# The turning quarter's forms in a Winograd MLP: two loads of 1 MB per form in place of four of 512 KB

## What is computed

```python
    h = rmsnorm(x, g_mlp_pre[l])
    f = jnp.square(jax.nn.relu(h @ w_up[l])) @ w_down[l]
    x = x + rmsnorm(f, g_mlp_post[l])
```

## Time and profile before

| what | us |
|---|---|
| three runs, median | 1496.4 |
| lowest, highest | 1494.74, 1497.96 |
| the profiled execution | 1498.13 |
| its span, first to last instruction | 1496.3 |

### The profile page before, as it was taken

The page is one execution under the profiler, slowest core; times in us unless marked ns, Lnnn a source line. Parts: engine busy times, 40 slices in busy tenths (PEclk is TensorE's granted clock), DMA queues, the critical chain, the costliest instruction groups (busy, mean ns, idle before and its releaser), DMA issues.

```text
span 1496.3 us, 18614 instructions
## 1 busy us (share of the span) xinstructions
PE 1467.2 (98%) x7222; PEld 1216.6 (81%) x7222; DVE 1056.6 (71%) x1709; ACT 529.9 (35%) x687; POOL 205.2 (14%) x316
## 2 busy tenths in 40 slices
PE   8999999999999999999999999899999999999987
PEld 7888778888888888888898887788888888888876
DVE  5768658657746724446756859597969696979868
ACT  4445744322123144221234432333334343434222
POOL 0000010041220212100100212302020202020100
PEclk9999999999999999999999999999999999999999
DMA  8301120242112236414533436837372737364535
GB/s 324 71 29 57 49 92 29 92 134 99 64 64 99 71 113 211 155 56 141 170 103 109 127 127 211 281 113 224 101 235 86 239 96 220 116 208 128 177 132 183
DMA packets 113907, 199.67 MB, mean 133 GB/s; under 512 B 15240, under 2 KB 57264, under 8 KB 113840
## 3 DMA queue, kind: packets, MB, share of 16 engines
q0 software_dynamic: 46288, 118.53, 25.2%
q1 hardware_dynamic: 67552, 80.23, 16.3%
HBM read 163.08 MB, written 35.65 MB: 133 GB/s over the span
## 4 chain that ended last, share of the span: by engine, by line
PE 80%; DVE 12%; issue 3%; DMA 2%; ACT 1%; POOL 1%; DVEq 0%; SPq 0%; ACTq 0%; POOLq 0%
PE bank L2003 48%; PE bank L2407 15%; PE bank L2427 8%; PE bank L2013 3%; PE bank L2043 2%; DVE acc L1832 1%; DVE ylo L1803 1%; DVE wlo L1799 1%; PE bank L2250 1%; DMA hTlo<-h_scratch 1%; PE bank L2136 1%; DMA raw<-in_w_up_dram 1%; DVE tok L1971 1%; DVE wlo L365 1%; PE bank L2265 1%
## 5 line engine op out<-in xcount | busy, mean ns | idle before, releaser
L2003 PE MATMUL bank<-hThi,whi 128*128 128x512 f32 x736 | 288.8, 392 | 0.5 <-DVE prob L1373 0.4
L2003 PE MATMUL bank<-hThi,wlo 128*128 128x512 f32 x736 | 286.5, 389 | 0.0
L2003 PE MATMUL bank<-hTlo,whi 128*128 128x512 f32 x736 | 286.5, 389 | 0.0
L1093 ACT ACTIVATE whi<-raw 128x1024 fp32r<-128x1024 f32 x91 | 95.3, 1055 | 191.6 <-DVE raw L1809 95.5
L2003 PEld LDWEIGHTS bank<-hThi,whi 128*128 128x128 f32 x736 | 138.2, 188 | 30.3 <-issue 1.8
L2003 PEld LDWEIGHTS bank<-hThi,wlo 128*128 128x128 f32 x736 | 138.2, 188 | 29.0
L2003 PEld LDWEIGHTS bank<-hTlo,whi 128*128 128x128 f32 x736 | 138.2, 188 | 28.0
L2407 PE MATMUL bank<-hThi,whi 128*128 128x512 f32 x336 | 131.6, 392 | 4.6 <-DVEq L1792 1.8
L1799 DVE TENSOR_TENSOR wlo<-raw,whi 128x1024 fp32r<-128x1024 f32 x91 | 110.8, 1218 | 34.5 <-ACT whi L1093 34.5
L2407 PE MATMUL bank<-hThi,wlo 128*128 128x512 f32 x336 | 130.8, 389 | 0.0
L2407 PE MATMUL bank<-hTlo,whi 128*128 128x512 f32 x336 | 130.7, 389 | 0.0
(11 more groups left out here) (402 smaller groups left out, 2752.3 us busy)
## 6 DMA issues: line engine op xcount, KB each, us to landing
hThi<-h_scratch POOLq DMA_DIRECT2D x42, 512.0 KB, 5.2
hTlo<-h_scratch POOLq DMA_DIRECT2D x42, 512.0 KB, 6.3
raw<-in_w_in_dram SPq DMA_DIRECT2D x34, 512.0 KB, 4.6
raw<-in_w_up_dram SPq DMA_DIRECT2D x32, 512.0 KB, 4.4
raw<-in_w_down_dram SPq DMA_DIRECT2D x32, 512.0 KB, 4.6
gate_scratch<-scr POOLq DMA_DIRECT2D x48, 256.0 KB, 2.3
tok<-gate_scratch POOLq DMA_DIRECT2D x24, 512.0 KB, 3.7
yhi<-h_scratch POOLq DMA_DIRECT2D x14, 512.0 KB, 6.6
```

The source lines that it names most:

```text
L1093: A.activation(w_slot(whi, place), source, ACT.Copy).then_inc(w_hi, 1)
L2003: ins = T.matmul(dst, lhs(k)[p], rhs(k)[q], start=start and k == 0 and i == 0, stop=stop and k == kt - 1 and i == 2)
```

## The change

`turn_load` waits for the old form's product alone (`pair_ready`), and then issues two loads, hi whole and lo whole, of 1 MB each. The wait on `turn_used` is gone from POOL; TensorE still counts it up. `turn_in[0]` now counts the landings of hi, `turn_in[1]` those of lo, and both parts of a product from the turning quarter wait on both: 32 for the four stores at the start, and 16 for each form loaded since. The kept forms are loaded as before.

```diff
             def turn_load(which, name, use, m):
-                pool.wait_ge(turn_used, use + 3 * m)
-                h_back(which, 0, turn, turn_in)
                 pair_ready(pool, name, m)
-                h_back(which, 1, turn, turn_in)
+                for hl, dst in enumerate(turn):
+                    g.dma_start(dst, h_dram[which, hl]).then_inc(turn_in[hl], 16)
...
                     use = ("uP1", "uP5", "uP4").index(name) if h is turn else None
                     for part in range(2):
                         if h is turn:
-                            pe.wait_ge(turn_in[part], 32 * (1 + use) + 96 * m)
+                            for hl in range(2):
+                                pe.wait_ge(turn_in[hl], 32 + 16 * use + 48 * m)
                         if h is kept2:
                             pe.wait_ge(kept_in[part], 64 + 32 * m)
```

## The result

The changed kernel takes 1501.6 us (median of 7 runs, 1499.53 to 1502.4) against 1496.4 before (1494.74 to 1497.96): a ratio of 1.0032, 95% interval 1.0020 to 1.0044. That is slower by 0.3%, and clear of no change. The forecast was 1500.5. The medians lie 5.2 us apart, and by the ratio it is 4.8 us. The profiled execution took 1501.87 with a span of 1500.1, so 3.7 us more than the profiled one of before. What the traces explain is this 3.7; the interval (3.0 to 6.6 us) holds all three numbers.

A forecast was written before the change was run, and what follows sets the result against it. TensorE, busy for 98% of the span, was taken to bound the kernel. First pass 2.72, clock 1.4, later passes 0 and extra waits 0 sum to 4.1 us on 1496.4: 1500.5, range 1497.1 to 1506.

The forecast's parts named there:

- Where the cost lies: Whole MLP: only the first pass's T1 form is waited for, before uP5; later passes show no wait on turning forms.
- The twelve matmuls, 2.72 us: First pass, uP5: twelve matmuls run behind the whole form's landing at 958.15 instead of ahead, 2.72 us later; bounds 0, 3.7.
- The clock, 1.4 us: First pass, uP5: TensorE's clock falls to half rate behind a 4.45 us pause, costing 1.4 us; bounds 0 and 1.7.
- Rival A: First pass: the clock holds behind the pause, so the cost is 2.7 us, 1499.1; chance 0.20.
- Later passes, 0: Later passes: whole forms land 9.0 to 9.8 us after issue, within about 10.3, costing 0; up to 5.2 us kept.
- Rival B: Later passes: forms are waited for too, 0.4 us for each of 13 uses, 1505.7 us; chance 0.20.
- One more wait at product starts, 0 to 0.3: TensorE, each half: one more wait, already met, costs 0, with up to 0.3 us kept for the six loop rounds.
- Rival C, the early landing: First pass: the merged loads land early, by 955.43, so not slower, a gain of at most 1.74 us; chance 0.08.

The follow-up runs named there:

- e1: Kernel before, half loads and waits by halves kept, but nothing issued until the old form's product is whole; ratio 1.0003.
- e2: Kernel before, loads unchanged, but TensorE waits for both halves of hi and lo before the first matmul of uP1, uP5, uP4; ratio 1.0026.
- e6: Changed kernel with TensorE's pass 0 written out ahead of the loop, and only the very first T1 form loaded and awaited by halves; ratio 1.0002.
- e4: Changed kernel with POOL's first loads reordered to T2, T1, T3 (T3 with its own count); 1492.99 us, ratio 0.9980 against before.
- e5: Changed kernel with TensorE's pass 0 written out ahead of the loop, nothing else; ratio 1.0025 against before, 1500.45 us.
- e7: Changed kernel, pass 0 written out, with twelve idle TensorE matmuls before the wait for pass 0's whole T1 form; 1498.86 us, ratio 1.0014 against before.
- e3: Kernel before, loads by halves, with POOL's first loads reordered to T2, T1, T3 (T3 with its own count); 1492.80 us, ratio 0.9973.
- e8: Changed kernel with each T1 form issued one product later, after uP2 in place of uP1; 1539.43 us, ratio 1.0277 against before.

## Why the prediction was right, step by step

**Where the cost lies: right.** Only the first pass's T1 is waited for. The parts alone (e1, e2), the first form alone (e6) and the order (e4) all say so.

**The twelve matmuls, 2.72 us: right, with the landing not quite where it was.** The start of uP7 moved from 961.01 to 964.48, by 3.47 us. It is 2.72 for the twelve matmuls that come behind the landing, 1.6 for the clock, and 0.8 less because this execution's form landed earlier (uP5 goes on at 957.35, not 958.15). Counted from pass 0's own first matmul, which starts 0.34 us later in the profile after, the landing is 1.1 us earlier. A single execution can't say whether the larger loads did this. The landing came 22.1 to 24.2 us after pass 0's start in the four traces with T1 of pass 0 in halves, issued as before (e2, e1, before, e6), and 22.3 to 22.4 in the three with it whole (after, e5, e7). So e2 has the early landing without any change of the loads, and a small gain by the larger ones is neither shown nor excluded.

One reading of the forecast is loose: 956.03 is the start of the twelfth matmul and not its end, which is 0.39 later and 1.74 before 958.15. The 2.72 does not depend on it.

**The clock, 1.4 us: right in kind, a little small.** uP5 takes 964.48 - 957.35 = 7.13 us where 24 x 0.227 and 0.1 for the restart would be 5.55: 1.6 us. The slow stretch began with the matmuls, so none of it lay inside the pause. The pause was 3.7 us and not 4.45, for the earlier landing, and sufficed. e7 gives 1.6 as well, by medians and by its trace. Rival A had 0.20 and did not come. The argument was thinner than its outcome: it went by the length of one earlier pause, and in e6 the clock fell behind pauses of 2.61 and 2.08 us, about as long as those of before that left it alone.

**Later passes, 0: right, with the landing mis-sized.** I had a whole form land 9.0 to 9.8 us after its issue, from the kept form's four loads; it lands after 7.9 by the medians. The step that was off is the row it was read from: four issues are not a measure for two. POOL's issue of 1 MB takes 0.75 us, hardly more than the 0.71 of 512 KB, so the range of 1.4 to 2.8 for a form is 1.5. In e1, where the same forms come by four loads in a row, the nineteen behind the first T1 take 9.0 to 10.8 us. The margin was 2.5 us in most passes, not 0.5 to 1.4. Rival B did not come, but T4 of pass 6 took 9.7 us and had 0.7 to spare, so the forecast's 0.5 to 1.4 was right for the slowest form. The larger loads helped here: by four loads that form took 10.8 us in e1. Awaited whole, it would have been about 0.4 us late, an estimate from e1's trace; no run joined the late issue with halves that are awaited whole.

**One more wait at product starts, 0 to 0.3: at the edge of the bounds.** From uP7 of pass 0 to the end of pass 6 TensorE slips by another 0.3 us (+3.47 to +3.77), at the starts of passes, where the waits that end with VectorE's additions to acc sum to 1.2 us (the list of waits above) instead of 0.6. The same sum is 0.4 to 0.6 in the three kernels with one wait per half (before, e1, e3) and 0.9 to 1.7 in the seven with two (after, e2, e4 to e8). That fits the further wait as the cause. It is not shown, since only e2 adds nothing but waits, its 0.9 is close to 0.6, and the times of whole executions can't tell 0.3 us.

**Rival C, the early landing:** the first form landed 0.9 us earlier in this execution (957.2 against 958.2), but it needed 2.7.

The trace's own sum is thus 2.72 + 1.6 - 0.8 + 0.3 = 3.8 us, the difference of the two spans. The other 1.5 of the 5.2 us between the medians lies in which executions were profiled: that of before was 1.7 us above its median, with its late landing, and that of after 0.3 above. What made the whole of that 1.7 is not known. e5, the same work, shows +3.7 and e2 +3.9. The forecast's 1500.5 is 1.1 below the measured 1501.6, and its sum of 4.1 lies between these numbers.

## What to carry to other kernels

A transfer split in halves buys its consumer half a product of slack, and this is worth nothing where the transfer has a margin. Where it has none, it is worth that half product (2.7 us here), and the slow clock on top if the longer stall brings it. So look for the one use with the longest queue ahead of it (here the first), and at the use with the slowest transfer (here T4 of pass 6), not at the average. There the better cure was neither halves nor whole loads but the order of the queue. Of the first three forms the one needed last had been sent first; putting it last gave 4 us and brought halves and whole loads within 1 us of each other. A stall of a few microseconds on TensorE should be priced with the slow clock behind it, here 1.6 us behind a stall of 3.7. A transfer that is moved later should be checked against what then runs beside it.

## What the runs showed of the hardware

**One load of 1 MB was cheaper than two of 512 KB issued by POOL in a row.** The issue costs 0.75 us against 0.71 each. In the timeline of e1 (four loads of 512 KB, B11 of pass 2) and its DMA list, the last landing is 2.1 + 7.9 = 10.0 us after the first issue; the same form takes 8.1 by two whole loads in the changed kernel. Form by form, over the nineteen behind the first T1, the two loads are whole 1.1 to 2.6 us sooner after the first issue. Of that, 1.4 us is that the last issue begins 0.7 us after the first and not 2.1.

```profile
1128.35 0.71 POOL L702 DMA_DIRECT2D hThi<-h_scratch  x1 [13.51 <-PE bank L2406]
...
1130.44 0.73 POOL L702 DMA_DIRECT2D hTlo<-h_scratch  x1
...
hTlo<-h_scratch POOLq DMA_DIRECT2D x1, 512.0 KB, 7.9
```

The Trainium skill (DMA: Bandwidth & Descriptors, Measured) advises 1 MiB and more per DMA, and the trace agrees that the larger loads are the faster ones here, 7.8 to 9.7 us for a form against 9.0 to 10.8; the share of the peak was not measured. It did not help this kernel, since nobody waited for the difference.

**The clock does not go by the length of one pause alone.** It stayed at 1.00 behind pauses of 2.20 and 1.74 us in the kernel before, of 1.91 and 1.33 in e1 and of 1.78 and 0.94 in e7; it fell behind 3.66, 3.47 and 3.61 (after, e2, e5) and behind 2.61 and 2.08 in the profiled e6. The stretch at 0.50 is 3.41 us in most cases and 6.83 in some, as in pass 2 of e8 (1123.10 to 1129.93). Behind the late pause of 3.8 us that every kernel has, the window of e3 is slow for 5.53 us from 1436.40 on, where that of before was slow for 3.41:

```profile
1436.40:1441.93 5.53, 5.45 (x13) 4.32 (x14) 5.50 (x4) 1.53 (x2) 0.00 (x0) 0.50 0.01 3
```

Half of the 2 us more of slow matmuls is 1 us, an estimate of what this alone moved between these two executions. That is not small beside the effects measured here, so a difference of one microsecond should be read from medians of many runs and not from two executions.
